# Delta layer of a hybrid decoder: sums of squares as two single-pass products, decay rows of all heads from one product, a shared buffer for v's front tiles

## What is computed

```python
qkv = silu(causal_dwconv(h @ w_in[...], conv_w))        # q, k: 8 heads x 128; v: 8 heads x 256
q, k = l2_norm(q), l2_norm(k)                           # x * rsqrt(sum(x * x) + EPS)
g = -exp(a_log) * softplus(a_logit + dt_bias)           # log decay of each step, one per head
...
g = jnp.cumsum(g, axis=-1)
decay = jnp.exp(jnp.where(causal, g[..., :, None] - g[..., None, :], -jnp.inf))
lower = jnp.where(strict, (k_beta @ k.T) * decay, 0.0)  # then a triangular solve
qk = (q @ k.T) * decay
...
# scan over chunks: v_new = u - w @ state; o = q @ state + qk @ v_new; state = ...
```

## Time and profile before

| | |
|---|---|
| median of 3 runs | 2372.68 us (2370.05 to 2373.39) |
| profiled execution: its own time | 2374.37 us |
| profiled execution: span of the trace | 2372.7 us, mean granted clock of TensorE 0.993 |
| busy, share of the span | PE 97%, PE weight load 81%, DVE 59%, ACT 52%, POOL 10% |
| delta layer | from about 38 us to about 950 us of the span |
| sums of squares (L889) | 32 products, 64 records of 592 ns |
| decay rows (L916) | 64 products, 128 records of 275 ns |

### The profile page before, as it was taken

One profiled execution on the slowest core, in us unless ns is written; L12 is line 12 of the kernel. 1 busy time (PEld: TensorE's weight loads), 2 busy tenths in 40 slices (PEclk: granted clock), 3 DMA queues, 4 the chain that ended last, 5 costly groups with the idle time before them and its releaser, 6 DMA issues. The chain is left out here.

```text
span 2372.7 us, 35061 instructions
## 1 busy us (share of the span) xinstructions
PE 2303.7 (97%) x11550; PEld 1924.8 (81%) x11550; DVE 1400.0 (59%) x2573; ACT 1234.4 (52%) x2517; POOL 244.6 (10%) x387
## 2 busy tenths in 40 slices
PE   7999999999999998799999999999999999999989
PEld 5788878888888877678788888888888888888877
DVE  5766657575757573786672836548283664828441
ACT  5556555555656564555545445454544545455430
POOL 1202121212112120650000000000000000000000
PEclk9999999999999999899999999999999999999999
DMA  4112130302121211778311212111121211111151
GB/s 136 40 51 75 36 80 23 88 26 77 38 65 40 63 44 34 260 253 282 119 27 48 60 36 62 36 45 36 46 61 36 62 36 45 36 48 59 52 211 49
DMA packets 274927, 173.15 MB, mean 73 GB/s; under 512 B 69692, under 2 KB 256212, under 8 KB 274804
## 3 DMA queue, kind: packets, MB, share of 16 engines
q1 hardware_dynamic: 274804, 171.60, 24.8%
HBM read 144.12 MB, written 27.45 MB: 72 GB/s over the span
## 5 line engine op out<-in xcount | busy, mean ns | idle before, releaser
L373 PE MATMUL b_front<-g_h_hi,wb_w_hi 128*128 128x512 f32 x1280 | 507.0, 396 | 3.0 <-PEq L1329 3.0
L373 PE MATMUL b_front<-g_h_lo,wb_w_hi 128*128 128x512 f32 x1280 | 508.5, 397 | 0.0
L373 PE MATMUL b_front<-g_h_hi,wb_w_lo 128*128 128x512 f32 x1280 | 508.2, 397 | 0.0
L373 PE MATMUL a_proj<-g_h_hi,wa_w_hi 128*128 128x512 f32 x784 | 322.8, 412 | 2.5 <-PEq L242 1.0
L373 PE MATMUL a_proj<-g_h_lo,wa_w_hi 128*128 128x512 f32 x784 | 322.4, 411 | 0.0
L373 PE MATMUL a_proj<-g_h_hi,wa_w_lo 128*128 128x512 f32 x784 | 316.6, 404 | 0.0
L373 PEld LDWEIGHTS b_front<-g_h_hi,wb_w_hi 128*128 128x128 f32 x1280 | 240.8, 188 | 50.9 <-issue 3.3
L373 PEld LDWEIGHTS b_front<-g_h_hi,wb_w_lo 128*128 128x128 f32 x1280 | 240.8, 188 | 47.5
L373 PEld LDWEIGHTS b_front<-g_h_lo,wb_w_hi 128*128 128x128 f32 x1280 | 240.9, 188 | 46.9
L1949 ACT ACTIVATE b_acc<-b_front,g_gains 128x512 f32<-128x512 f32 x96 | 66.1, 689 | 279.8 <-DVE b_qk L2241 215.2
L2124 DVE TENSOR_TENSOR wb_w_lo<-wb_raw,wb_w_hi 128x1024 fp32r<-128x1024 f32 x79 | 96.0, 1215 | 139.6 <-ACT wb_w_hi L1897 139.6
(11 more groups left out here) (295 smaller groups left out, 4463.8 us busy)
## 6 DMA issues: line engine op xcount, KB each, us to landing
wb_raw<-in_b_w_in_dram SPq DMA_DIRECT2D x80, 512.0 KB, 3.9
p_w_raw<-in_a_w_out_dram SPq DMA_DIRECT2D x64, 512.0 KB, 4.2
wa_raw<-in_a_w_in_dram SPq DMA_DIRECT2D x48, 512.0 KB, 4.2
a_out<-a_og SPq DMA_DIRECT2D x64, 128.0 KB, 1.8
p_a_raw<-a_out SPq DMA_DIRECT2D x64, 128.0 KB, 5.0
a_zx<-inverse_tiles SPq DMA_DIRECT2D x16, 384.0 KB, 4.5
u_tiles<-a_u SPq DMA_DIRECT2D x8, 512.0 KB, 3.2
p_x<-in_x_dram SPq DMA_DIRECT2D x4, 1024.0 KB, 8.0
```

The source lines that it names most:

```text
L373: last = pe.matmul(out, w[:, k, :], a[:, k, ks], start=(n == 0), stop=(n == 23))
```

## The change

Three things.

1. Sums of squares. ACT now squares a half twice, once rounded to float32r (`sq_hi`) and once in float32 (`sg`). DVE subtracts (`sq_lo` = `sg` - `sq_hi`), in slots 8, 11, 14 and 17, behind whatever it has to do in its slots up to there. PE waits for DVE's `sq_low` in place of ACT's `sq`, and multiplies ones by `sq_hi` and by `sq_lo`, one pass each, in the same slots as before.
2. Decay rows. In the setup PE makes the cumulated log decays of all heads and tiles as rows by one more product; DVE splits them in a high and a low part; SP writes these to DRAM and reads them back as `rows` (32 partitions by 512). Each head's two groups of four float32 products become one float32r product each, of a broadcast column that picks the head (`pick`, one more small POOL copy per head) with `rows`.
3. v's tiles 0 to 3 of both heads in flight share one buffer (`v_front`), tiles 4 to 7 keep two. The space goes to `sq_hi` and `sq_lo`. No wait is added for it.

```diff
         kq = m_.sb("kq", [P, 2, T, 2, P])
-        v = m_.sb("v", [P, 2, T, DV])
+        v_front = m_.sb("v_front", [P, TH, DV])
+        v_back = m_.sb("v_back", [P, 2, TH, DV])
+        sq_hi = m_.sb("sq_hi", [P, HALF], F32R)
+        sq_lo = m_.sb("sq_lo", [P, HALF], F32R)
...
         cols = m_.sb("cols", [P, 7, T, H])
-        hc = m_.sb("hc", [P, 2, 7, T])
+        hc = m_.sb("hc", [P, 2, 6, T])
...
         neg_a = m_.sb("neg_a", [P, H])
+        rows = m_.sb("rows", [4 * H, HALF], F32R)
+        pick = m_.sb("pick", [4 * H, 2, 2], F32R)
+        row_hi, row_lo = (dec[0:T * H, c, :].bitcast(F32R) for c in range(2))
...
+
+        rows_dram = nc.dram_tensor("decay_rows", [2, T * H * P], F32, kind="Internal").ap()
...
         convs, taps = sem("convs"), sem("taps")
-        sq, nsum, rs, rss, kqn = sem("sq"), sem("nsum"), sem("rs"), sem("rss"), sem("kqn")
+        sq, sq_low = sem("sq"), sem("sq_low")
+        nsum, rs, rss, kqn = sem("nsum"), sem("rs"), sem("rss"), sem("kqn")
...
+        def v_half(p, half):
+
+            return v_back[:, p] if half else v_front[:, :, :]
+
+        def v_tile(p, t):
+            return v_half(p, t // TH)[:, t % TH, :]
...
                             load(n + 1, 0)
+                    if m is None and s == SETUP_DECAYS + 2:
+                        sp.wait_ge(totals, 3)
+                        for c, part in enumerate((row_hi, row_lo)):
+                            sp.dma_start(rows_dram[c].rearrange("(r i) -> r i", i=P), part.bitcast(F32)).then_inc(inv_zero, 16)
+                        sp.wait_ge(inv_zero, 64)
+                        for c in range(2):
+                            for half in range(2):
+                                at = (2 * c + half) * H
+                                src = rows_dram[c].rearrange("(a t h i) -> a h t i", a=2, h=H, i=P)[half]
+                                sp.dma_start(rows[at:at + H, :].bitcast(F32).rearrange("h (t i) -> h t i", i=P), src
+                                             ).then_inc(inv_zero, 16)
...
                 pool.wait_ge(og_s, n * T)
-                pool.tensor_copy(hc[:, p], cols[:, :, :, bass.ds(n, 1)].rearrange("p a t o -> p a (t o)")
+                pool.tensor_copy(hc[:, p], cols[:, 0:C_LOG, :, bass.ds(n, 1)].rearrange("p a t o -> p a (t o)")
+                                 ).then_inc(hc_s, 1)
+                pool.tensor_copy(pick[:, p, :], cols[0:4 * H, C_LOG, 0:2, bass.ds(n, 1)].rearrange("r a o -> r (a o)")
...
                             act.wait_ge(act_out, n * HALVES + (q + 1 + 2))
+                            act.activation(sq_hi[:, :], acc[:, q % 2], ACT.Square)
...
                             c = q // 2 - 2
-                            act.activation(v[:, p, (q % 2) * TH:(q % 2 + 1) * TH, c * P:(c + 1) * P],
+                            act.activation(v_half(p, q % 2)[:, :, c * P:(c + 1) * P],
...
                 pe.matmul(turn[:, 256:256 + T * H], g.tri[:, :], log, start=True, stop=True)
-                pe.matmul(turn[:, 384:384 + T * H], g.ones[:, :], log, start=True, stop=True).then_inc(setup, 1)
+                pe.matmul(turn[:, 384:384 + T * H], g.ones[:, :], log, start=True, stop=True)
+                pe.matmul(gram[0:T * H, 0:P], log, g.tri[:, :], start=True, stop=True).then_inc(setup, 1)
...
                                 pe.wait_ge(vn_s, m * T + (t + 1))
-                                pe.matmul(new[:, :], zf[:, t], r[:, :] if t else v[:, pm, 0, :], start=True, stop=True
+                                pe.matmul(new[:, :], zf[:, t], r[:, :] if t else v_tile(pm, 0), start=True, stop=True
...
                             q = (s - 8) // 3
-                            pe.wait_ge(sq, n * 4 + (q + 1))
+                            pe.wait_ge(sq_low, n * 4 + (q + 1))
                             turn_is_free(("sum", q))
-                            pe.matmul(turn[:, :], g.ones[:, :], sg[:, q % 2], start=True, stop=True).then_inc(nsum, 1)
+                            pe.matmul(turn[:, :], g.ones_r[:, :], sq_hi[:, :], start=True, stop=False)
+                            pe.matmul(turn[:, :], g.ones_r[:, :], sq_lo[:, :], start=False, stop=True).then_inc(nsum, 1)
...
                             else:
-                                pe.wait_ge(hc_s, n * 5 + 5)
+                                pe.wait_ge(hc_s, n * 6 + 6)
...
                                     pe.wait_ge(ut, n * (T // 2))
-                            for t in range(TH):
-                                last = pe.matmul(gram[:, t * P:(t + 1) * P], spread(hc[:, p, C_LOG, half * TH + t], 1, P),
-                                                 g.tri[:, :], start=True, stop=True)
-                            last.then_inc(row_mm, 1)
+                            if isinstance(n, int) and n == 0:
+                                pe.wait_ge(inv_zero, 128)
+                                pe.wait_ge(totals, 3)
+                            pe.matmul(gram[:, :], spread(pick[:, p, half], 1, P), rows[:, :],
+                                      start=True, stop=True).then_inc(row_mm, 1)
...
             dve.tensor_tensor(tmp[:, 1], tmp[:, 0], cols[:, C_CUM], ALU.subtract).then_inc(setup, 1)
+            picks = g.ident[0:4 * H, 0:4 * H].rearrange("r (c a h) -> r c a h", c=2, a=2)
+            dve.tensor_tensor(cols[0:4 * H, C_LOG, 0:2, :], picks[:, 0], picks[:, 1], ALU.add)
+            dve.tensor_copy(row_hi, gram[0:T * H, 0:P]).then_inc(totals, 1)
+            dve.wait_ge(totals, 2)
+            dve.tensor_tensor(row_lo, gram[0:T * H, 0:P], row_hi.bitcast(F32), ALU.subtract).then_inc(totals, 1)
...
                             dve.wait_ge(ks_mm, m * (T - 1) + t)
-                            dve.scalar_tensor_tensor(r[:, :], step[:, 0], hc[:, pm, C_NEXP, t:t + 1], v[:, pm, t, :],
+                            dve.scalar_tensor_tensor(r[:, :], step[:, 0], hc[:, pm, C_NEXP, t:t + 1], v_tile(pm, t),
...
                                 split_low(n * UNITS + (1 + j), slot_of(j % UNITS))
+                        q, k = divmod(s - 8, 3)
+                        if 0 <= q < 4 and k == 0:
+                            dve.wait_ge(sq, n * 4 + (q + 1))
+                            dve.tensor_tensor(sq_lo[:, :], sg[:, q % 2], sq_hi[:, :].bitcast(F32), ALU.subtract
+                                              ).then_inc(sq_low, 1)
                         if s == 4:
-                            dve.wait_ge(hc_s, n * 5 + 5)
+                            dve.wait_ge(hc_s, n * 6 + 6)
```

## The result

| | before | after |
|---|---|---|
| median of 5 runs each, same chip | 2372.68 us | 2381.90 us (2381.13 to 2383.08) |
| ratio, 95% interval | | 1.0040 [1.0029, 1.0051] |
| profiled execution, span | 2374.37, 2372.7 us | 2382.36, 2380.6 us |
| mean granted clock | 0.993 | 0.991 |

The change costs 9.2 us, 0.4%. The forecast was +3.8 us; 2381.9 lies inside its range of 2367 to 2384, near the upper end, and slower by over 0.2% had the largest of the three chances (0.46).

The account below looks back on a forecast made before the run. PE was taken to bound the delta layer, busy 110.63 of 113.00 us a head. Seven fronts with a chain at +1.0 and head 0 at +2.8 give +3.8 on the median of 2372.68: 2376.5 us, range 2367 to 2384.

Parts of the forecast that it names:

- fronts with a chain: Seven fronts: sums +1.46 and row products -1.32 give +0.14 us each, +1.0 together.
- head 0: Front without a chain: late subtractions put the fourth sum's successor +3.4 us later, 0.6 swallowed, net +2.8.
- What the pair saves: PE's sums of squares: an unhindered pair takes 0.46 for 0.86 us, saving 0.40, 32 times: 12.8 us.
- What the pair waits for: PE waits for DVE's queued subtraction; the four sums net -0.25, +0.82, +0.85, +0.04 us, +1.46 per head.
- What the row product saves: PE's decay rows: one product takes 0.23 in place of 0.89 us, saving 0.66, 16 times: 10.6 us.
- a product is not as short as taken: Rival on 32 rows of weights and the broadcast operand: +0.2 us each, +3, 2380; chance 0.04.
- Costs taken as nothing: ACT's second square, DVE's extra subtraction, setup, v's shared buffer and the DRAM trip add no time.
- The low part is in time: Rival: DVE subtracts before PE arrives; 2349 us, or 2359 with no stall at second and third alone; chance 0.14.
- The stall spreads: Rival: DVE's idle time in slots 12 and 15 vanishes; seven heads by 0.8 to 1.5, 2382 to 2387 us; chance 0.14.
- The DRAM trip holds head 0: Rival: the DRAM trip or SP's order holds head 0 by +4 to +8, 2381 to 2385 us; chance 0.08.
- The stalls bring the clock down: Rival: 14 long stalls each bring a stretch at 1.2 GHz, costing 1.7 us; +24, 2400 us; chance 0.03.

Follow-up runs that it names:

- e3: The change, but both products of a pair read sq_hi and PE waits only for ACT's square; 2364.42 us, 11.1 below the kernel before.
- e10: The change with PE's pairs one slot later, rows and pick padded to 128 partitions, 28 semaphore increments a front; 2355.89 us, 15.6 below the kernel before.
- e4: The change with rows and pick padded from 32 to 128 partitions; 2383.40 us, 7.9 above the kernel before.
- e6: The change with PE's pairs taken one slot later (9, 12, 15, 18); 2368.74 us, 6.1 below the kernel before.
- e1: The change with the decay rows as before, so only sums as pairs and v's shared buffer; 2388.17 us, 12.7 above the kernel before.
- e8: The change with DVE's subtraction earlier, inside the convolution, 128 partitions and 28 semaphore increments a front; 2361.70 us, 13.1 below the kernel before.
- e2: The change with the sums of squares as before, so only the decay rows and v's shared buffer; 2375.77 us, 0.3 above the kernel before.
- e9: The change with 28 semaphore increments a front added to PE's program that nobody waits for; 2380.04 us, 8.5 above the kernel before.

## Why the prediction came out as it did

Its direction and its mechanism (PE waits for a low part that DVE's order makes late) were right, its size 5.4 us too small. In the traces the fronts with a chain gave +2.7 for +1.0 and head 0 +1.4 for +2.8; that these two add up to 4.1, next to the forecast's 3.8, is errors that cancel. The edges gave +4.9, the tail -2.1, the second layer +1.0, and the medians differ by 1.2 us more than the two profiled executions. By its own steps:

- **What the pair saves** (0.86 against 0.46): right, 0.47 in e3 and e10.
- **What the pair waits for**: right in the place, the order and the size. In slots 11 and 14 PE waits 1.03 and 1.06 us. The second net stall is +0.73 for 0.82 foreseen, the third +0.76 for 0.85, the fourth +0.03 for 0.04. The first is -0.52 for -0.25: the pair hardly waits there (0.51 to 0.54 long), and the stretch ahead of it gives 0.15 more. The four together are +1.0 for +1.46, so this step put the cost 0.46 a front too high.
- **What the row product saves** (0.66): the term that was mis-sized. It measured 0.28 in the change, 0.66 in e4. The step took the 0.23 of a full product in a stream; the rival "a product is not as short as taken" (chance 0.04) named the 32 rows, with 0.2 each where 0.38 was measured. Two of them cost 0.76 more per front than was forecast, and with the 0.46 of the sums that leaves +0.30 a front; seven of them are 2.1, less 0.4 in the last front: +2.7 for +1.0.
- **Head 0**: what follows the fourth sum stands at 87.68 for 88.71 forecast and 85.26 before (as the prediction counts; the trace has its record at 84.85 already, but the next one only at 85.49). That it is 1.0 earlier than forecast is luck of the run: the first product is reached at 61.10, before at 62.20. From there to the fourth sum the stalls (0.66, 1.74, 2.12, 1.20) add +3.5, as worked out (+3.4). Later 1.0 is swallowed and not 0.6: +1.4 net for +2.8.
- **Costs taken as nothing**: ACT's second square, the setup and the DRAM trip held. The trip's six DMAs are issued from 49.57 to 53.4 us, the rows are used at 72.00 without a wait. The shared buffer of v shows no new wait; it was not tried alone.
- **What was not in the working at all**: the +4.9 us in the stretches with the loop's branch. The first line of rows 1 spans such an edge: it has 113.00 us for a head, where one without an edge takes 110.5, and the prediction uses both figures without asking for the difference. The one place where before already waited on `issue` (0.5 us, the fifth row of PE's waits) was not taken up either. In 2 to 3 and 6 to 7, moreover, a 16 KB fetch falls on the store of u (306.31 and 757.23 us). In SP's order of time the issue behind the first comes after 4.6 us (5.1 behind the second), before after 3.2 (302.41 to 305.62):

```profile
304.69 0.37 SPq L580 DMA_DIRECT2D u_tiles<-a_u  x1
309.34 0.62 SPq L584 DMA_DIRECT2D a_bd<-u_tiles  x1
```

The output store behind that is late too, and with it DVE's a_og, in DVE's order of time. PE's turn of k then waits for a_og, 0.2 us here and 0.8 in 6 to 7:

```profile
312.40 0.42 DVE L1083 TENSOR_TENSOR a_og<-a_turn,a_z 128x256 f32<-128x256 f32 x1 [1.27 <-DMA a_out<-a_og]
```

The rivals. "The low part is in time" did not occur. Its prices of 2359 and 2349 lie 14 and 23 us below before; where the low part is in time in the fronts with a chain, e3 has -11.1, e6 -6.1 and e10 -15.6 us. "The stall spreads" fell: DVE idles 2.13 us behind the subtraction, and the fourth stall stayed at 0.31. "The DRAM trip holds head 0" fell. "The stalls bring the clock down": 14 stalls of about 1 us came with no stretch at 1.2 GHz, and in the change the one such stretch starts within the `issue` wait of 2.17 us. Behind a longer stall one did come: in e1 and e4 head 0's third sum waits 2.16 and 2.17 us for the low part, and a stretch at 1.2 GHz starts with the end of that wait (79.1 and 78.8 us; in e3 one starts at 81.6, behind 1.9 us for a_dec). From 60 to 880 us the clock falls eleven times in all traces together, each time within a wait of PE of 1.8 to 2.8 us or up to 1.2 us behind it; about as many other waits of that size have no such stretch. The Trainium skill, "TensorE: Matmul & The Clock Gate", A second HAM failure mode, tells of a kernel in which frequent micro-idles between groups of products made the clock oscillate. By that rule the 14 stalls would; the trace does not agree here.

On the row product the same page of the Trainium skill (Why this matters for your kernels) says that a single product over 32 rows takes the same time as one over 128. The traces do not agree: the records are 495 ns in the change and 388 in e4, and between neighbours of full height the 32-row product held the stream up for 0.38 us more. The distances are wider on both sides of it (0.32 ahead and 0.42 behind, in e4 0.23 and 0.23). Why is not shown.

## What to carry to other kernels

When an edit moves a wait from one engine to another, lay the two queues side by side in time: DVE was busy for 60% and had 2 us of idle time right behind the subtraction, and PE still waited 1 us for it. Both remedies work, and nearly alike: a slot of slack on the waiting side leaves 108.0 us a head (e10), moving the producer, which makes something else late, 108.3 (e8). The totals do not tell them apart.

Read the loop's edges apart from its period, and treat an `issue` wait of half a microsecond as a warning: in e2, which shortens PE's body by 58 instructions, it was 2.1 us at each edge. An instruction count restored by increments is no sure cure (e9, e10). Try an operand at full height where its neighbours are, even if most of it is zeros: here the short form cost 0.38 us more a product.

## What was not expected of the hardware

- A float32r product of 512 columns over 32 partitions, between full-height ones, costs about 0.61 us of the stream where one over 128 partitions costs 0.23.
- PE goes on 1.6 to 2.2 us behind the end of a 16 KB instruction fetch at the loop's branch, at all 26 edges (before 344.91 to 346.68, change 349.49 to 351.33). Of the 26 edges, those with a fetch 3.4 to 4.2 us ahead of the branch had the next one 1.1 to 1.7 us behind it, all others 2.0 to 3.2. What decides between them stays open.
- A 16 KB instruction fetch during the 512 KB store of u went with 4.3 to 5.1 us between two of SP's issues, 14 times in six traces; the 90 other stores of the thirteen traces have 3.2 to 3.4. It was not tried apart.
